# A new row plan for the attention, merge and expert stages of a mixer-and-experts layer on one core

## The reference

```python
x = layer_norm(ALPHA * x + hybrid_mixer(x, ...))
x = layer_norm(ALPHA * x + peer_ffn(x, ...))

# hybrid_mixer: h = x @ w_in; forgetting attention (8 heads, all earlier keys), sliding-window
# attention (window 128), pooling and convolution; then
merged = (gates[:, :, 0] * (y_fox @ p_fox) + gates[:, :, 1] * (y_pool @ p_pool)
          + gates[:, :, 2] * (y_conv @ p_conv) + gates[:, :, 3] * (y_swa @ p_swa))
return merged @ w_out

# peer_ffn: per token and head the 16 best of 16384 experts (two top-16 of 128 keys, then a top-16
# of their sums) -> ib (128 experts a token), gb (softmax of their scores)
act = gelu(einsum('cd,ced->ce', xb, u_tab[ib]))
return einsum('ce,ced->cd', gb * act, v_tab[ib])
```

## Time and profile before

| | us |
|---|---|
| median of 3 runs | 3737.34 |
| lowest, highest | 3729.81, 3761.74 |
| the profiled execution | 3710.51 |
| its span | 3708.7 |
| busy in it: TensorE, VectorE, ScalarE, POOL | 3169.6, 2640.0, 862.0, 1542.0 |

### The profile page before, as it was taken

The page is one execution under the profiler, slowest core; times in us unless marked ns, Lnnn a source line. Parts: engine busy times, 40 slices in busy tenths (PEclk is TensorE's granted clock), DMA queues, the critical chain, the costliest instruction groups (busy, mean ns, idle before and its releaser), DMA issues.

```text
span 3708.7 us, 40267 instructions
## 1 busy us (share of the span) xinstructions
PE 3169.6 (85%) x14161; PEld 1745.7 (47%) x14161; DVE 2640.0 (71%) x5092; ACT 862.0 (23%) x2077; POOL 1542.0 (42%) x1321
## 2 busy tenths in 40 slices
PE   7579889988988895886999898998998998889960
PEld 6458545755655564532444443544443443334420
DVE  6745449976666556876788996959758764546788
ACT  7444212122222121200211652825510000000000
POOL 5100001124544423444254434434436567776463
PEclk9779999998888797997999999999999999999985
DMA  8369434357777646977499989999999999999996
GB/s 293 137 234 369 174 130 137 109 162 255 262 248 260 227 166 247 398 269 299 174 391 348 322 310 348 333 359 327 351 398 326 409 354 338 335 332 389 408 410 238
DMA packets 313257, 1073.16 MB, mean 289 GB/s; under 512 B 36704, under 2 KB 62944, under 8 KB 309216
## 3 DMA queue, kind: packets, MB, share of 16 engines
q0 software_dynamic: 170704, 606.75, 44.9%
q1 hardware_dynamic: 101904, 363.16, 26.4%
q10 hardware_dynamic: 40448, 100.68, 7.5%
HBM read 931.52 MB, written 138.94 MB: 289 GB/s over the span
## 4 chain that ended last, share of the span: by engine, by line
DMA 17%; POOL 11%; PE 10%; DVE 9%; issue 5%; DVEq 1%; ACT 0%; ACTq 0%; POOLq 0%
PE ps L1789 7%; DMA rows<-v,expert_ids 6%; POOL rows L146 5%; DMA turned_rows<-v,expert_ids 4%; DMA rows<-u,expert_ids 4%; POOL hidden_sums L1754 4%; DVE row_sums L181 3%; POOL turned_rows L146 2%; DVE rows L175 2%; DMA h_side_kept<-mixer_state 1%; DVE branches L1948 1%; PE ps L122 1%; PE ps L121 1%; PE ps L120 1%; DMA mixer_state<-u_t 1%
## 5 line engine op out<-in xcount | busy, mean ns | idle before, releaser
L146 POOL DMA_INDIRECT rows<-u,expert_ids x471 | 570.4, 1211 | 870.5 <-DVE hidden_sums L175 745.9
L1789 PE MATMUL ps<-turned_rows,mixer_state 128*128 128x512 f32 x2048 | 899.0, 598 | 4.9 <-DMA mixer_state<-u_t 4.2
L146 POOL DMA_INDIRECT rows<-v,expert_ids x525 | 575.1, 1095 | 659.3 <-DVE row_sums L181 538.9
L181 DVE SCALAR_TENSOR_TENSOR row_sums<-rows,hidden_sums,row_sums 128x1024 f32<-128x1024 f32 x518 | 655.8, 1281 | 246.4 <-DMA rows<-v,expert_ids 242.6
L1826 PE MATMUL ps<-shared_64k 128*128 128x512 f32 x1536 | 680.9, 606 | 57.9 <-DVE shared_64k L1956 57.9
L1789 PEld LDWEIGHTS ps<-turned_rows,mixer_state 128*128 128x128 f32 x2048 | 388.2, 192 | 476.2 <-issue 469.5
L1826 PEld LDWEIGHTS ps<-shared_64k 128*128 128x128 f32 x1536 | 297.7, 195 | 441.2 <-issue 441.2
L175 DVE CUSTOM_DVE_ANT_0 rows<-rows,x_first 128x1024 f32<-128x1024 f32 x256 | 306.2, 1222 | 41.3 <-DMA rows<-u,expert_ids 38.8
L120 PE MATMUL ps<-x_hi_t_b,shared_64k 128*128 128x384 f16 x912 | 309.2, 339 | 17.8 <-DMA shared_64k<-w_pairs_kept 17.8
L175 DVE CUSTOM_DVE_ANT_0 rows<-rows,branches 128x1024 f32<-128x1024 f32 x215 | 261.4, 1219 | 67.9 <-DMA rows<-u,expert_ids 64.3
L121 PE MATMUL ps<-x_lo_t_b,shared_64k 128*128 128x384 f16 x912 | 308.3, 338 | 0.0
(11 more groups left out here) (573 smaller groups left out, 4993.9 us busy)
## 6 DMA issues: line engine op xcount, KB each, us to landing
mixer_state<-u_t ACTq DMA_DIRECT2D x128, 512.0 KB, 6.9
shared_64k<-v SPq DMA_DIRECT2D x128, 512.0 KB, 6.8
rows<-strips SPq DMA_DIRECT2D x32, 768.0 KB, 7.2
h_kept<-branches ACTq DMA_DIRECT2D x32, 768.0 KB, 9.8
shared_64k<-weights_kept SPq DMA_DIRECT2D x32, 768.0 KB, 9.7
shared_64k<-h_kept SPq DMA_DIRECT2D x32, 768.0 KB, 13.5
shared_64k<-s_pairs_kept SPq DMA_DIRECT2D x32, 512.0 KB, 5.7
rows<-w_t SPq DMA_DIRECT2D x30, 512.0 KB, 5.6
```

Of the source, the lines that this page charges most:

```text
L146: nc.gpsimd.indirect_dma_start(row_tile(M, n), None, A["u" if r < NSEL else "v"], bass.IndirectOffsetOnAxis(ap=M["idx"][:, c, e:e + 1], ax ...
L181: nc.vector.scalar_tensor_tensor(acc[:, e % 2, :], src, hid[:, c % 2, e:e + 1], acc[:, e % 2, :], ALU.mult, ALU.add).then_inc(used, 1)
L1789: m = pe.matmul(ps[:, 4 + u % 4, 0:UT], uk[u % 4][:, k, :], x1t[:, k, :], start=k == 0, stop=k == KD - 1)
```

## The change

The rows are dealt out anew. A head unit gets one row more (`unit_rows`), a step of the sliding-window part 11 in place of 6, a merge item one in place of two, a block of the first pass 2.9 in place of 3.1, and a block of the second pass 2.4 in place of 2.2. The third one-hot window moves from block 86 to 96. The choice of chunk 3 takes blocks 78 to 92 in place of 82 to 105, that of chunk 4 ends at block 141 in place of 150, and ScalarE's exponents for chunk 3 follow block 93 in place of 106. What is computed stays as it is.

```diff
@@ -101,12 +101,12 @@
     if u >= N_UNIT_B:
         return 3
-    return 2 if bare_unit(u) else (3, 4, 4, 4, 5, 5)[u // 2 % GB.nc]
+    return 3 if bare_unit(u) else (4, 5, 5, 5, 6, 6)[u // 2 % GB.nc]
 
 
 FILL_STEPS = [s for s in range(N_UNIT_B + 2 + 2 * (GB.nc + 1)) if not bare_unit(s)][:FILL]
-ATT_ROWS = spans_of(PROJ_ROWS[-1][1], [0] + [unit_rows(u) for u in range(N_UNIT_B + 2)] + [6] * (GB.nc + 1))
-MERGE_ROWS = spans_of(ATT_ROWS[-1][1], [2] * ITEMS + [6, 6, 6, 5, 3, 0])
+ATT_ROWS = spans_of(PROJ_ROWS[-1][1], [0] + [unit_rows(u) for u in range(N_UNIT_B + 2)] + [11] * (GB.nc + 1))
+MERGE_ROWS = spans_of(ATT_ROWS[-1][1], [1] * ITEMS + [6, 6, 6, 5, 3, 0])
@@ -1589,10 +1589,10 @@
-WINDOW_AT = [30, 58, 86]
-ROWS_U_BLOCK = 3.1
-ROWS_V_BLOCK = 2.2
-CHOICE_SPAN = {5: (0, 20), 6: (24, 47), 7: (52, 75), 3: (82, 105), 4: (112, 150)}
+WINDOW_AT = [30, 58, 96]
+ROWS_U_BLOCK = 2.9
+ROWS_V_BLOCK = 2.4
+CHOICE_SPAN = {5: (0, 20), 6: (24, 47), 7: (52, 75), 3: (78, 92), 4: (112, 141)}
@@ -1619,7 +1619,7 @@
-EXP_BLOCK = {5: 21, 6: 48, 7: 76, 3: 106}
+EXP_BLOCK = {5: 21, 6: 48, 7: 76, 3: 93}
```

## The result

The changed kernel takes 3811.0 us, median of 4 runs (3786.4 to 3823.4); the kernel before takes 3745.8, median of 4 (3729.8 to 3761.7). The ratio is 1.0166 (95% interval 1.0094 to 1.0238): slower by over 1%, and outside the predicted range. Its profiled execution has a span of 3821.6 us against 3708.7.

The account below looks back on a forecast made before the run. VectorE and DMA had idle room in the attention; TensorE bounded most of the first pass and the second from 3361 us. Terms +12 + 34 - 20 + 0 + 10 + 6 - 12 = +30 gave 3740 to 3767, forecast 3755 us, range 3700 to 3800.

Parts of the forecast that it names:

- Head units: +12 us: Attention head units: 46 more rows mostly hide in VectorE's idle time, costing 12 us, bounds 0 and 57.
- VectorE sets the attention: Slower rival: all attention rows exposed, +57 in units and +59 in window part, 3837 us; half, 3787, counted; chance 0.29.
- Window part: +34: Sliding-window steps: rows set the step at 25 us, +18, and the end adds +16; bounds +9 and +59.
- Merge: -20: Merge: one row fewer an item lets TensorE set 4.1 us, -16; five rows behind the loop, -4.
- First pass: +10: First pass: window beginnings +2, pressed choice of chunk 3 +8; bounds -15 and +20 us.
- Start of the second pass: +6: Second pass before its first product: scores load queues behind the 8 MB store, +6 us, bounds -10 and +20.
- punctual-load rival: Second pass start, block 112: scores load doesn't queue behind the store, -14 in place of +6, 3735 us; chance 0.12.
- Second pass and tail: -12: From the second pass's first product to the end: 839 us against 851, bounds -30 and +5.
- Pre: Second pass, first product to first value gather: 108 us for 45 rows in place of 145 for 63.
- Z: Value stretch, first to last value gather: POOL full, stays 358 us.
- post: Second pass, last value gather to last product: 126 rows in place of 85, at 2.23 us each, 281 us.
- faster rival: Whole kernel: attention hides its rows and the tail's gain is kept, -45, 3692 us; chance 0.12.

Follow-up runs that it names:

- first_b: The kernel before, same row plan, with VectorE's table rows in a head unit moved ahead of the wait for TensorE's values: ratio 0.9854.
- the repeated trace: The whole changed kernel measured and traced a second time, against the kernel before: ratio 1.0156, median 3780.6 us.
- q01: The kernel before with one row more only in head units of query blocks 0 and 1, 16 rows: ratio 1.0020.
- first_spread: The kernel before with rows ahead of the values wait in head units and the 128 value gathers spread over 160 rows: ratio 0.9787, 3653.95 us.

## Why the prediction was wrong

The failed step is *Head units: +12 us*. It said that much of VectorE's idle time "is VectorE waiting for TensorE's values (80.5 us in 28 waits), and a row there is free". The rows stand behind that wait in VectorE's order; they delay the next reduction, and 57 of the 80.5 us of waiting stay (`first_b` fills all but 7 of them with rows that stand ahead of it). It measured +65, beyond the stated upper bound of 57: that bound counted VectorE's passes alone, not the gathers, whose waits grew by 28 us. The rival "VectorE sets the attention" had +57 here, near to what was measured, and I gave it 0.29 and half its size. But its condition, that VectorE's own work fills a unit's period, isn't met: its work (318 us) and its waits for rows (47) fill 365 of 469 us. All rows were exposed while VectorE still idled.

*Window part: +34* had the mechanism right, the rows set the step, and its size wrong: +58, against that rival's +59. A step is 31.2 us, not 25. 3.1 us of the difference are the gathers, and 3.2 TensorE's values at the low clock level: I took matmul durations from rows at full clock for a TensorE that the change makes wait. The end, +16, measured +18.

*Merge: -20* measured -32 (-22 in the loop, -10 behind it), beyond the bound of -26. The loop runs at 120.9 / 31 = 3.90 us an item; I had set TensorE's busy time as the floor, at 4.1. The floor was named rightly (TensorE is busy for 119.9 of 121.2 us of the changed loop) and set 5% too high. *Scores: 0* measured -1.

*First pass: +10* measured -13. TensorE's waits where a window begins were meant to grow and fell, from 47.6 to 41.6 us in all:

```profile
PE ps L1807 <- ACT branches L1879: 41.6, 6, 14.1
```

The +8 for the pressed choice of chunk 3 didn't come: VectorE was 24.0 us behind TensorE at block 92, yet the wait of the window at block 96 was 15.4 us, as the 15.2 at block 86 before. The waits account for 6 of the 13 us; the rest is within what U varies by between traces.

*Start of the second pass: +6* measured -3. The load behind the store came as predicted (30.0 us), which ends the punctual-load rival. VectorE lagged by 24.6 us at block 112 (26 forecast); then it held the lag, 26.5 at block 126 and not 36. What I added for more waits for rows didn't come.

*Second pass and tail: -12* measured -12, and its parts are right too, so this is no luck. *Pre* is -39 (-37 forecast), Z is +1 (0), *post* +87 (from the first to the last product 108 + 358 + 281 = 747 us were forecast, and 745 measured), the tail -59 (-63). (The last product stands at row 1116, not 1115.) The rate behind the value stretch is 405 GB/s again, above the 358 of the Trainium skill ("DMA: Bandwidth & Descriptors", "Where 436 GB/s comes from"). So the tail shrank by 59 us, as it looked from the profile, and the blocks in front of it took 49 of them back.

In sum: forecast +30; measured +62 in the repeated trace. Units (+53 over), window part (+24), merge (-12), first pass (-23) and start (-9) make up the difference. Errors of both signs stand in this sum: the first pass, the start and the merge hide 44 us of the 77 that the attention missed. The faster rival is refuted: a finish follows the previous one by 27 to 32 us in both traces of the changed kernel, not by under 22.

## What to carry to other kernels

An engine's idle time in front of a wait can hide only work that stands ahead of that wait in the engine's own order, and only until the wait is filled. Ask of every "free" instruction which wait it would fill, and what is queued behind it. Moving side work between stages is a trade of prices, and here they ran 0.6 to 0.9 us a row in the merge and the first pass, 1.3 in the tail, 1.4 to 1.6 in the head units and the window part, and 1.9 to 2.2 in front of and behind the value stretch. The change put 46 and 37 rows into the attention and 42 behind the value stretch. Of the dear places it relieved only one, by 18 rows; the other rows came from where they cost 0.7 and 1.3. Moving no row at all to another stage, but the rows' place in the unit, gained 1.5%.

## What was not expected of the hardware

In these traces a TensorE that waits pays twice. After 4.61 us of waiting its 32 value matmuls took 7.00 us in place of 3.76, and the whole of the head units' matmuls was 20 us shorter when the waits went (362 to 343 us busy, clock 0.88 to 0.95).

The profiled execution of the changed kernel holds a further stretch of this kind in the value stretch, which its repeat does not show at this length (0.90 over its Z):

```profile
3120.00:3150.00 30.00, 23.99 (x51) 9.98 (x50) 15.18 (x25) 0.31 (x1) 23.10 (x23) 0.90 0.80 276
3150.00:3226.00 76.00, 37.87 (x39) 11.34 (x39) 32.05 (x26) 0.00 (x0) 56.16 (x54) 0.50 0.71 224
3226.00:3434.00 208.00, 183.09 (x390) 76.89 (x390) 98.70 (x77) 0.00 (x0) 141.37 (x134) 0.91 0.89 316
```

TensorE stays at 0.50 for 76 us while it is busy half of the time, and POOL issues 54 gathers as elsewhere. Z is 383.4 us in this execution and 367.8 in the repeat. What started it is open. It is not the only one: `q01` has 0.59 from 3335 to 3398 us, late in its value stretch, with TensorE busy for 35 of 63 us, and `first_spread` the stretch named above. A value stretch read from one execution can be off by some 15 us for it.
